# A two-layer encoder kernel: sixteen column sums as two rounded passes, later weight splits, smaller first pieces

## The chip, the cores and the metric

The kernel runs on one core of a Trainium2 chip. The time is the device time of one execution in microseconds (us). Shorter is better. A core has five engines with instruction queues of their own: TensorE (PE in the profile) multiplies matrices, VectorE (DVE) and ScalarE (ACT) do elementwise work and reductions, GpSimd (POOL) is idle here, and SyncE (SP) issues the weight transfers. PEld is the loading of a matmul's stationary operand, which overlaps PE.

## The reference

Two layers of an encoder on 272 tokens (16 learned meta tokens and 256 inputs) of width 2048. Everything is float32.

```python
def hybrid_layer(x, ...):
    h = rms_norm(x, norm_w)
    proj = jnp.einsum('bld,dn->bln', h, w_in)
    (aq, ak, av, ag, bq, bk, bv, bg, cq, ckv, ckr, cg, du, dg) = jnp.split(proj, split_points, axis=-1)
    ya = diff_attention(aq, ak, av, ...)      # A: 4 heads, two softmax maps each
    yb = axial_gqa(bq, bk, bv, ...)           # B: 4 query heads, 2 key heads
    yc = latent_attention(cq, ckv, ckr, ...)  # C
    yd = multiscale_pool(du, ...)             # D
    y = jnp.concatenate([ya * silu(ag), yb * silu(bg), yc * silu(cg), yd * silu(dg)], axis=-1)
    return x + jnp.einsum('bln,nd->bld', y, w_out)
```

What the change touches is in branch A, where every half head (64 of the 128 features of a tile) of q and k is normalized before the rotation:

```python
def rms_norm(x, w):
    y = x32 * lax.rsqrt(jnp.mean(x32 * x32, axis=-1, keepdims=True) + EPS)

q = rms_norm(q_raw.reshape(b, l, A_HEADS, 2, A_QK_DIM), q_norm_w)
k = rms_norm(k_raw.reshape(b, l, A_HEADS, 2, A_QK_DIM), k_norm_w)
...
p = softmax32(jnp.einsum('bqhmd,bkhmd->bhmqk', qb, k), scale)
w = p[:, :, 0] - lam * p[:, :, 1]
o = einsum('bhqk,bkhd->bqhd', w, v);   o = rms_norm(o, subln_w) * (1.0 - lambda_init)
```

## The kernel before

Everything is kept transposed: features on the 128 partitions, tokens along the free axis (272 columns, or 256 in the layer that no longer needs the meta tokens). Weights stream from memory in chunks of 128 x 1024 float32 (512 KB) in the order of their use. A layer has 129 slots with a chunk each, the two layers 258. Four chunks make a pair of output tiles, a chunk holding 4 k-tiles of 128 rows for both.

A product of float32 precision is made of three rounded passes. ACT rounds a chunk to `w_hi` (`split`, L1039), DVE subtracts to get `w_lo` (`split`, L1348), and PE runs for each k-tile and output tile hi·hi (L736), x-low·w-high (L737) and x-high·w-low (L738), 24 matmuls to a chunk. There are 3 raw buffers and 4 of `w_hi` and `w_lo` each. A chunk's matmuls wait for both halves of its split, and its transfer into a raw buffer waits for the `w_lo` of the chunk three before.

Between the chunks PE does what attention needs: scores (`score`, L907), transposes of probabilities (`p_turn`, L922 and L926), products with v (`pv`, L943), sums of squares down the partitions (`rope_stat` L862 and others; `sub_stat` L951). A finished tile is taken by ACT (`lift`, L1066) and scaled by DVE (`rescale`, L1356). A tile of aq or ak is then squared by ACT (`rope_pre`, L1111), summed by PE (`rope_stat`, one matmul of the float32 squares with the constant `halves`, which the trace records as x2), turned by DVE meanwhile (`rope_turn`, L1388 to L1393), and multiplied by the inverse root, which ACT makes in two steps (L1138, L1140) and DVE applies (`rope_fin`, L1431). An attention step n has on DVE its maximum (`s_max`, L1508 and L1509) and its scaling (`s_scale`, from L1517), on ACT its two exponentials (`s_exp`, L1207) and the copies of turned probabilities (`p_out`, L1220 and L1222). The heads' outputs are normalized by `sub_pre`, `sub_stat` and `sub_fin` (L1454, L1456), and split again by `y_split` (L1438).

Each engine runs its instructions in an order fixed when the kernel is built. `make_plan` gives every stage a place, its slot plus the number for its kind in `AT_TENSOR`, `AT_SCALAR` or `AT_VECTOR` (plus an exception from `MOVED`), and sorts by it. An engine that has to wait for one stage waits with all the stages behind it.

At the start SP issues chunk 0 in two halves, alternating with the first two halves of a quarter of x, then chunks 1 to 3 in whole. ACT and DVE split the first half of chunk 0 (`split_half`), then two k-tiles of x (`x_half`: `h_hi` L1020, `h_lo` L1328), and so on; `x_first` brings k-tiles 4 to 7, 8 to 11 and 12 to 15.

Of the kernel before, what the change touches and what calls it, by code (L numbers as in the profile page):

```python
# [140 lines left out]

def make_plan(at_engine):
# [8 lines left out]
    for n in (0, 1):  # L151
        plan += [(-11, 2 * n, ("split_half", n)), (-11, 2 * n + 1, ("x_half", n))]
# [4 lines left out]
    plan += [(-5, 0, ("x_first", 0, 1)), (-3, 0, ("x_first", 0, 2)), (2.9, 0, ("x_first", 0, 3))]  # L157
# [4 lines left out]
    for l in range(DEPTH):  # L162
# [105 lines left out]
def build(nc, xt, w_stream, params, lam_rows, consts, out):  # L268
# [31 lines left out]
    sq = sb("sq", [128, 4, L])  # L300
    rn = sb("rn", [128, L])
# [197 lines left out]
    for stg in vector_plan:  # L499
# [7 lines left out]
        if stg[0] == "sq_sum":  # L507
# [219 lines left out]
    def _(pe):  # L727
# [965 lines left out]
```

## Time and profile before

| | |
|---|---|
| median of 3 runs | 904.98 us (904.94 to 906.03) |
| the profiled execution's own time | 905.02 us |
| its span | 903.24 us |
| granted TensorE clock | 0.999 of full speed |
| PE busy | 895.9 us, 99% of the span |
| DVE busy | 639.5 us, 71% |
| ACT busy | 566.5 us, 63% |
| DMA | 143.8 MB, a mean of 159 GB/s |

The span is the stretch from the first to the last recorded instruction of the profiled execution; 1.8 us of its time lie around it. Matmuls are pipelined: a dense one is recorded as 0.29 us, but the next starts some 0.125 us later. So what a matmul costs is read from the starts of its neighbours and not from its own duration. Times in a timeline count from the start of the span.

### The profile page before, as it was taken

How to read it: one execution, taken by the hardware profiler on the slowest of the kernel's cores; microseconds unless marked ns; L12 is line 12 of the kernel's file. 1: busy time of each engine (PE TensorE's matmuls, PEld its weight loads, DVE VectorE, ACT ScalarE, POOL GpSimd, SP SyncE). 2: the span in 40 equal slices, each digit the busy share in tenths (PEclk: the TensorE clock that was granted, in tenths of full speed). 3: DMA queues.
4: the chain of work that ended last, by engine and by line, in shares of the span. 5: the costliest groups of instructions: out<-in, count | busy, mean ns of one | idle time of the engine just before them, and what ended most of it. 6: DMA issues, size and time to landing. Idle time of an engine off the chain costs nothing.

```text
span 903.2 us, 18071 instructions
## 1 busy us (share of the span) xinstructions
PE 895.9 (99%) x7070; PEld 860.0 (95%) x7070; DVE 639.5 (71%) x1074; ACT 566.5 (63%) x986; POOL 0.2 (0%) x4
## 2 busy tenths in 40 slices
PE   8999999999999999999999999999999999999998
PEld 7999998998999999999999999999999999999998
DVE  7785887778777776766665659887687667766552
ACT  7678756577666667745454588556686666665331
POOL 0000000000000000000000000000000000000000
PEclk9999999999999999999999999999999999999999
DMA  8754333343434443445455544334435344445561
GB/s 333 264 197 140 134 140 137 124 136 115 145 139 143 139 149 130 147 147 190 172 199 186 188 176 151 118 120 176 149 97 184 140 141 157 152 158 187 187 217 64
DMA packets 22996, 143.83 MB, mean 159 GB/s; under 512 B 2560, under 2 KB 4736, under 8 KB 6528
## 3 DMA queue, kind: packets, MB, share of 16 engines
q1 hardware_dynamic: 22768, 142.64, 44.4%
q8 instruction: 56, 0.92, 0.4%
q14 instruction: 28, 0.23, 0.1%
q10 hardware_dynamic: 144, 0.04, 0.1%
HBM read 140.58 MB, written 2.10 MB: 158 GB/s over the span
## 4 chain that ended last, share of the span: by engine, by line
PE 97%; ACT 1%; DMA 1%; SPq 0%; DVE 0%; issue 0%; ACTq 0%; DVEq 0%
PE dense L736 27%; PE dense L738 26%; PE dense L737 26%; PE s_ps L907 4%; PE o_ps L943 4%; PE norm_ps L862 2%; PE t_ps L922 2%; DMA raw<-w_stream_dram 1%; ACT w_hi L1039 1%; PE swap_ps L738 0%; PE norm_ps L738 0%; PE norm_ps L737 0%; PE swap_ps L737 0%; PE swap_ps L736 0%; PE norm_ps L736 0%; PE norm_ps L951 0%
## 5 line engine op out<-in xcount | busy, mean ns | idle before, releaser
L736 PE MATMUL dense<-h_hi,w_hi 128*128 128x272 f32 (+2 forms) x1440 | 427.1, 297 | 2.3 <-DVE h_lo L1328 2.3
L738 PE MATMUL dense<-h_hi,w_lo 128*128 128x272 f32 (+2 forms) x1440 | 412.7, 287 | 0.0
L737 PE MATMUL dense<-h_lo,w_hi 128*128 128x272 f32 (+2 forms) x1440 | 410.9, 285 | 0.0
L1348 DVE TENSOR_TENSOR w_lo<-raw,w_hi 128x1024 fp32r<-128x1024 f32 (+1 forms) x256 | 312.0, 1219 | 86.5 <-ACT w_hi L1039 80.3
L1039 ACT ACTIVATE w_hi<-raw 128x1024 fp32r<-128x1024 f32 (+1 forms) x256 | 270.3, 1056 | 70.4 <-PE dense L738 56.1
L736 PEld LDWEIGHTS dense<-h_hi,w_hi 128*128 128x128 f32 x1440 | 271.3, 188 | 7.9 <-issue 2.8
L737 PEld LDWEIGHTS dense<-h_lo,w_hi 128*128 128x128 f32 x1440 | 271.4, 188 | 1.2
L738 PEld LDWEIGHTS dense<-h_hi,w_lo 128*128 128x128 f32 x1440 | 271.1, 188 | 0.0
L736 PE MATMUL dense<-y_hi,w_hi 128*128 128x272 f32 (+1 forms) x500 | 143.6, 287 | 0.2
L738 PE MATMUL dense<-y_hi,w_lo 128*128 128x272 f32 (+1 forms) x500 | 142.7, 285 | 0.0
L737 PE MATMUL dense<-y_lo,w_hi 128*128 128x272 f32 (+1 forms) x500 | 142.4, 285 | 0.0
L736 PEld LDWEIGHTS dense<-y_hi,w_hi 128*128 128x128 f32 x500 | 94.3, 189 | 1.4 <-ACT q_st L1090 0.6
L738 PEld LDWEIGHTS dense<-y_hi,w_lo 128*128 128x128 f32 x500 | 94.3, 189 | 0.0
L737 PEld LDWEIGHTS dense<-y_lo,w_hi 128*128 128x128 f32 x500 | 94.1, 188 | 0.0
L1066 ACT ACTIVATE row<-dense 128x272 f32<-128x272 f32 (+2 forms) x80 | 31.5, 394 | 71.5 <-PE dense L738 70.8
L1508 DVE TENSOR_REDUCE stat<-s_ps 128x1 f32<-128x272 f32 (+1 forms) x80 | 35.1, 439 | 35.1 <-PE s_ps L907 33.1
L1356 DVE TENSOR_TENSOR row<-row,rinv 128x272 f32<-128x272 f32 (+2 forms) x80 | 34.9, 437 | 28.4 <-ACT row L1066 26.6
L1138 ACT ACTIVATE rn<-norm_ps,eps_c 128x272 f32<-128x272 f32 (+1 forms) x50 | 24.2, 484 | 42.0 <-PE norm_ps L862 30.0
L1207 ACT ACTIVATE probs<-s_ps,stat 128x272 f32<-128x272 f32 (+1 forms) x80 | 38.9, 486 | 14.0 <-DVE stat L1509 11.6
L1337 DVE TENSOR_TENSOR x<-x,dense 128x272 f32<-128x272 f32 (+1 forms) x28 | 12.0, 429 | 46.7 <-PE dense L738 46.7
L943 PE MATMUL o_ps<-p_t,v_st 128*128 128x128 f32 (+1 forms) x288 | 38.2, 278 | 0.3 <-ACT p_t L1222 0.3
L907 PE MATMUL s_ps<-k_st,q_st 64*128 64x272 f32 (+1 forms) x240 | 37.6, 417 | 0.0
(175 smaller groups left out, 808.1 us busy)
## 6 DMA issues: line engine op xcount, KB each, us to landing
raw<-w_stream_dram SPq DMA_DIRECT2D x128, 1024.0 KB, 4.8
out_dram<-x SPq DMA_DIRECT2D x8, 256.0 KB, 4.7
x<-xt_dram SPq DMA_DIRECT2D x3, 544.0 KB, 8.9
raw<-w_stream_dram SPq DMA_DIRECT2D x3, 512.0 KB, 7.6
con<-consts_dram SPq DMA_DIRECT2D x1, 984.0 KB, 7.8
x<-xt_dram SPq DMA_DIRECT2D x2, 272.0 KB, 4.8
raw<-w_stream_dram SPq DMA_DIRECT2D x2, 256.0 KB, 4.6
d_w<-consts_dram SPq DMA_DIRECT2D x2, 256.0 KB, 5.3
```

What stands on the lines that cost most here:

```text
L736: nc.tensor.matmul(ps, whi, xhi, start=first, stop=False)
L737: nc.tensor.matmul(ps, whi, xlo, start=False, stop=False)
L738: return nc.tensor.matmul(ps, wlo, xhi, start=False, stop=last)
L907: mm = nc.tensor.matmul(s_ps[m][0:nq, 0:L], queries[half, q:q + nq], keys[half, :], start=n_part == 0, stop=n_part == len(parts) - 1)
L943: mm = nc.tensor.matmul(o_ps[:, c:c + nq], v_st[:, b, v_columns(vh)], p_t[:, 4 if b == 2 else 2 * m + b, 0:nq], start=b == 0, stop=b == 2)
L1039: signal(nc.scalar.activation(w_hi[:, g % RING, 0:n], raw[:, e % RAW, CHUNK * half:CHUNK * half + n], ACT.Copy), hi_ready, g + 1)
L1066: signal(nc.scalar.activation(tile_place(l, p, j), ps[:, 0:L - tile_from(l, kind, j)], ACT.Copy), lifted, scaled_no[(l, p, j)])
L1138: signal(nc.scalar.activation(rn[:, t0:L], norm_ps[:, t0:L], ACT.Ln, scale=1.0 / width, bias=eps_c[:, 0:1]), norm_taken, n + 1)
L1207: signal(nc.scalar.activation(probs[0:nq, k % 2, m, :], s_ps[m][0:nq, 0:L], ACT.Exp, bias=stat[0:nq, 2 + m:3 + m], scale=SCALE[b], accum_o ...
L1348: signal(nc.vector.tensor_tensor(w_lo[:, g % RING, 0:n], raw[:, e % RAW, CHUNK * half:CHUNK * half + n], w_hi[:, g % RING, 0:n].bitcast(F3 ...
L1356: signal(nc.vector.tensor_tensor(out_, out_, rinv[:, tile_from(l, PAIRS[p][0], j):L], ALU.mult), scaled, scaled_no[(l, p, j)])
L1508: link(nc.vector.reduce_max(stat[0:nq, m:m + 1], s_ps[m][0:nq, 0:L], AX.X))
```

## The change

**The sums.** The 16 sums of aq and ak (4 tiles each in 2 layers) are made from two rounded parts. ACT copies the squares to a rounded `sq_hi` behind the square, DVE subtracts to get `sq_lo` (a new stage `sq_low` at place 0.6), and PE runs two passes over a rounded copy of `halves`, one slot later than the single sum stood. `rope_fin` is one slot later too, and `sub_slot` keeps the sums of head outputs out of the two slots in which these now stand.

**Copies of probabilities.** `p_out` on ACT goes from place 0.56 to 0.105, directly ahead of `rope_pre` (0.11).

**Late weight splits.** On DVE the `split` of slots 27 to 94 of each layer goes from 0.71 to 1 + 0.491 + 0.03, behind the `s_scale` of the slot after.

**The start.** Chunk 0 is transferred and split in k-tiles 0, 1 and 2-3. The first quarter of x comes in the same pieces and is issued by ACT, ahead of its table load; SP issues weights and the rest of x. `x_first` is cut finer.

```diff
+FIRST = [(0, 1), (1, 2), (2, 4)]
...
-                 y_split=0.66, xscale=0.283, sub_pre=0.439, x_out=0.55, p_out=0.56, gate=0.65, s_exp=0.579,
+                 y_split=0.66, xscale=0.283, sub_pre=0.439, x_out=0.55, p_out=0.105, gate=0.65, s_exp=0.579,
...
-AT_VECTOR = dict(sq_sum=0.2, rope_mid=0.25, rope_turn=0.65, s_max=-0.418, lam_dot=-0.35, sub_fin=-0.345, rope_fin=-0.34, lat_fin=0.055, head_out=0.17,
+AT_VECTOR = dict(sq_sum=0.2, sq_low=0.6, rope_mid=0.25, rope_turn=0.65, s_max=-0.418, lam_dot=-0.35, sub_fin=-0.345, rope_fin=-0.34, lat_fin=0.055, head_out=0.17,
...
+LATE_SPLITS = (27, 95)
...
-            plan.append((slot + at_engine[kind] + MOVED.get(stage, 0), len(plan), stage))
+            place = at_engine[kind] + MOVED.get(stage, 0)
+            if kind == "split" and at_engine is AT_VECTOR and LATE_SPLITS[0] <= stage[2] < LATE_SPLITS[1]:
+                place = 1 + at_engine["s_scale"] + 0.03
+            plan.append((slot + place, len(plan), stage))
...
-    plan += [(-5, 0, ("x_first", 0, 1)), (-3, 0, ("x_first", 0, 2)), (2.9, 0, ("x_first", 0, 3))]
+    plan += [(-6.5, 0, ("x_first", 4, 6)), (-5, 0, ("x_first", 6, 8)), (-3, 0, ("x_first", 8, 12)),
+             (2.9, 0, ("x_first", 12, 16))]
...
-                    at(s, ("rope_stat", l, kind, i0 + j))
-                    at(s + 1, ("rope_fin", l, kind, i0 + j))
+                    at(s, ("sq_low", "rope", l, kind, i0 + j))
+                    at(s + 1, ("rope_stat", l, kind, i0 + j))
+                    at(s + 2, ("rope_fin", l, kind, i0 + j))
...
-            taken |= {pair_slot(p) + 4, pair_slot(p) + 5}
+            taken |= {pair_slot(p) + 5, pair_slot(p) + 6}
...
-            sp.dma_start(x[:, 2 * n:2 * n + 2, :], xt[:, 2 * n:2 * n + 2, :]).then_inc(s_x[0] if n else s_x_half, 16)
...
+            if key not in ("aq", "ak"):
+                sums = nc.tensor.matmul(norm_ps[:, t0:L], halves, sq[:, 2 * half, t0:L], start=True, stop=True)
             else:
...
+                nc.tensor.matmul(norm_ps[:, t0:L], sums_of[:, :], sq_hi[:, half, t0:L], start=True, stop=False)
+                sums = nc.tensor.matmul(norm_ps[:, t0:L], sums_of[:, :], sq_lo[:, half, t0:L], start=False, stop=True)
...
+            act.dma_start(x[:, 0:1, :], xt[:, 0:1, :]).then_inc(s_x_part[0], 16)
             act.dma_start(par[:, :], params).then_inc(s_par, 16)
+            act.dma_start(x[:, 1:2, :], xt[:, 1:2, :]).then_inc(s_x_part[1], 16)
+            act.dma_start(x[:, 2:4, :], xt[:, 2:4, :]).then_inc(s_x[0], 16)
             nc.scalar.preload_act_table_set("natural_log_exp_and_others")
...
+            signal(nc.scalar.activation(sq_hi[:, half, t0:L], sq[:, 2 * half, t0:L], ACT.Copy), pre_done,
                    pre_no[("rope_pre", l, key, i)])
...
+        def sq_low(what, l, key, i):
+
+            t0, half = rope_from(l, key), parity("rope_stat", l, key, i)
+            dve.wait_ge(pre_done, pre_no[("rope_pre", l, key, i)])
+            signal(nc.vector.tensor_tensor(sq_lo[:, half, t0:L], sq[:, 2 * half, t0:L],
+                                           sq_hi[:, half, t0:L].bitcast(F32), ALU.subtract), summed,
+                   sum_no[(what, l, key, i)])
```

Three places show what moved. **DVE in layer 0, slots 58 to 61, before.** `w_lo<-raw,w_hi` is a weight split, the 16-row lines are an attention step's, the `tab` and `k_st` lines turn and scale the tile ak3. From the split of chunk 60 on:

```order
L1348 TENSOR_TENSOR w_lo<-raw,w_hi 128x1024
L1508 TENSOR_REDUCE stat<-s_ps 16x1 x2
L1509 TENSOR_SCALAR stat<-stat 16x2
L1388 STREAM_SHUFFLE tab<-row 128x272
L1389 SCALAR_TENSOR_TENSOR tab<-tab,par,con 128x272
L1391 SCALAR_TENSOR_TENSOR k_st<-row,par,con 128x272
L1393 TENSOR_TENSOR k_st<-k_st,tab 128x272
L1431 TENSOR_TENSOR k_st<-k_st,rn 128x272
L1348 TENSOR_TENSOR w_lo<-raw,w_hi 128x1024
L1517 RECIPROCAL stat<-stat 16x2
```

After, from the same split on:

```order
L1377 TENSOR_TENSOR w_lo<-raw,w_hi 128x1024
L1545 TENSOR_REDUCE stat<-s_ps 16x1 x2
L1546 TENSOR_SCALAR stat<-stat 16x2
L1409 TENSOR_TENSOR sq_lo<-sq,sq_hi 128x272
L1425 STREAM_SHUFFLE tab<-row 128x272
...
L1468 TENSOR_TENSOR k_st<-k_st,rn 128x272
L1554 RECIPROCAL stat<-stat 16x2
L1557 TENSOR_TENSOR stat<-stat,neg_lam 16x1
L1558 TENSOR_SCALAR probs<-probs,stat 16x272
L1559 SCALAR_TENSOR_TENSOR probs<-probs,stat 16x272
L1377 TENSOR_TENSOR w_lo<-raw,w_hi 128x1024
```

The split of chunk 61, the last line of the second list, now stands behind the four scaling instructions of the attention step, and there is a subtraction more ahead of it. The split of chunk 59 has moved in the same way behind the scaling of the step before.

**DVE in layer 1, slot 79, before.** The `tab` and `yt` lines are the normalization of a head's output, `sq<-sq` adds the squares of two bq tiles and the four lines behind it begin their rotation (chunk 208 is this layer's slot 79):

```order
L1356 TENSOR_TENSOR row<-row,rinv 128x256 x2
L1454 SCALAR_TENSOR_TENSOR tab<-o_ps,sub_w,rn 128x256
L1456 TENSOR_TENSOR yt<-tab,g_st 128x256
L1348 TENSOR_TENSOR w_lo<-raw,w_hi 128x1024
L1374 TENSOR_TENSOR sq<-sq 128x256
L1404 SCALAR_TENSOR_TENSOR tab<-row,par,con 128x2x256
L1405 SCALAR_TENSOR_TENSOR q_st<-row,par,con 128x2x256
L1407 TENSOR_TENSOR q_st<-q_st,tab 128x2x256
```

After:

```order
L1385 TENSOR_TENSOR row<-row,rinv 128x256 x2
L1491 SCALAR_TENSOR_TENSOR tab<-o_ps,sub_w,rn 128x256
L1493 TENSOR_TENSOR yt<-tab,g_st 128x256
L1403 TENSOR_TENSOR sq<-sq 128x256
L1441 SCALAR_TENSOR_TENSOR tab<-row,par,con 128x2x256
L1442 SCALAR_TENSOR_TENSOR q_st<-row,par,con 128x2x256
L1444 TENSOR_TENSOR q_st<-q_st,tab 128x2x256
L1377 TENSOR_TENSOR w_lo<-raw,w_hi 128x1024
```

The split of chunk 208 has gone from directly behind the head's output to behind the sum and the rotation.

**ACT at the start, before:**

```order
L977 DMA par<-params_dram 128x84
L978 ACT_TABLE_LOAD
L983 ACTIVATE w_hi<-raw 128x512
L1020 ACTIVATE h_hi<-x,par 128x272 x2
L983 ACTIVATE w_hi<-raw 128x512
L1020 ACTIVATE h_hi<-x,par 128x272 x2
L989 ACTIVATE w_hi<-raw 128x512 x2
L1039 ACTIVATE w_hi<-raw 128x1024
L1020 ACTIVATE h_hi<-x,par 128x272 x4
```

After:

```order
L998 DMA x<-xt_dram 128x544
L999 ACT_TABLE_LOAD
L1004 ACTIVATE w_hi<-raw 128x256
L1044 ACTIVATE h_hi<-x,par 128x272
L1004 ACTIVATE w_hi<-raw 128x256
L1044 ACTIVATE h_hi<-x,par 128x272
L1004 ACTIVATE w_hi<-raw 128x512
L1044 ACTIVATE h_hi<-x,par 128x272 x2
L1011 ACTIVATE w_hi<-raw 128x512 x2
L1044 ACTIVATE h_hi<-x,par 128x272 x2
L1063 ACTIVATE w_hi<-raw 128x1024
L1044 ACTIVATE h_hi<-x,par 128x272 x2
```

Three transfers more are issued ahead of the table load (the last is shown), the first split covers one k-tile in place of two, and two of the four k-tiles of x that stood behind the split of chunk 2 (L1039, now L1063) stand ahead of it.

## Rows read from the trace of the kernel before

**Rows 1.** Page, part 4: the chain that ended last, share of the span by engine

```profile
PE 97%; ACT 1%; DMA 1%; SPq 0%; DVE 0%; issue 0%; ACTq 0%; DVEq 0%
```

**Rows 2.** Waits of PE: waiting tile, waited-for line, us in total, times, longest

```profile
PE dense L736 <- DVE h_lo L1328: 2.3, 3, 1.7
```

**Rows 3.** PE timeline, 272 columns wide: start, duration, engine, line, operation, tiles

```profile
89.76 0.29 PE L738 MATMUL dense<-h_hi,w_lo 128*128 128x272 f32 x1
89.89 0.62 PE L862 MATMUL norm_ps<-sq,con 128*128 128x272 f32 x2
...
90.47 0.28 PE L737 MATMUL dense<-h_lo,w_hi 128*128 128x272 f32 x1
```

**Rows 4.** PE timeline, 256 wide, at chunk 208

```profile
743.83 0.28 PE L738 MATMUL dense<-h_hi,w_lo 128*128 128x256 f32 x1
...
744.19 0.47 PE L736 MATMUL dense<-h_hi,w_hi 128*128 128x256 f32 x1
744.50 0.28 PE L737 MATMUL dense<-h_lo,w_hi 128*128 128x256 f32 x1
```

**Rows 5.** PE timeline of the start, around the two pauses

```profile
9.07 0.36 PE L736 MATMUL dense<-h_hi,w_hi 128*128 128x272 f32 x1 [0.17 <-DVE h_lo L1328]
...
13.55 0.29 PE L738 MATMUL o_ps<-h_hi,w_lo 128*128 128x272 f32 x1
14.25 0.36 PE L736 MATMUL dense<-h_hi,w_hi 128*128 128x272 f32 x1 [0.41 <-DVE h_lo L1328]
```

**Rows 6.** ACT timeline of the start: chunk 2's rounding

```profile
11.18 1.06 ACT L1039 ACTIVATE w_hi<-raw 128x1024 fp32r<-128x1024 f32 x1 [1.15 <-DMA raw<-w_stream_dram]
```

**Rows 7.** DVE timeline of the start: the low parts of x tiles 4 to 7

```profile
13.60 2.11 DVE L1328 SCALAR_TENSOR_TENSOR h_lo<-x,par,h_hi 128x272 fp32r<-128x272 f32 x4
```

**Rows 8.** Page, part 6: transfers, count, KB each, us from issue to landing

```profile
raw<-w_stream_dram SPq DMA_DIRECT2D x2, 256.0 KB, 4.6
```

**Rows 9.** DVE timeline, layer 0: from the scaling of step 10 to chunk 61's split

```profile
220.92 0.17 DVE L1517 RECIPROCAL stat<-stat 128x2 f32<-128x2 f32 x1
...
222.26 0.46 DVE L1388 STREAM_SHUFFLE tab<-row 128x272 f32<-128x272 f32 x1
...
224.31 0.44 DVE L1431 TENSOR_TENSOR k_st<-k_st,rn 128x272 f32<-128x272 f32 x1
224.79 1.22 DVE L1348 TENSOR_TENSOR w_lo<-raw,w_hi 128x1024 fp32r<-128x1024 f32 x1
226.04 0.89 DVE L1508 TENSOR_REDUCE stat<-s_ps 16x1 f32<-16x272 f32 x2
...
227.17 0.46 DVE L1388 STREAM_SHUFFLE tab<-row 128x272 f32<-128x272 f32 x1
...
229.69 1.23 DVE L1348 TENSOR_TENSOR w_lo<-raw,w_hi 128x1024 fp32r<-128x1024 f32 x1
```

**Rows 10.** ACT timeline at the same place: the second exponential, and the square

```profile
220.17 0.49 ACT L1207 ACTIVATE probs<-s_ps,stat 128x272 f32<-128x272 f32 x1
...
222.85 0.43 ACT L1111 ACTIVATE sq<-row 128x272 f32<-128x272 f32 x1
```

**Rows 11.** PE timeline: the first matmul of chunk 61

```profile
232.50 0.39 PE L736 MATMUL dense<-h_hi,w_hi 128*128 128x272 f32 x1
```

**Rows 12.** DVE timeline, layer 1: the maximum of step 7

```profile
668.93 0.17 DVE L1509 TENSOR_SCALAR stat<-stat 128x2 f32<-128x2 f32 x1
```

**Rows 13.** PE timeline: the first matmul of chunk 189

```profile
678.02 0.37 PE L736 MATMUL dense<-h_hi,w_hi 128*128 128x272 f32 x1
```

**Rows 14.** DVE timeline, layer 1: splits around the rotation, chunk 208's first

```profile
741.60 1.23 DVE L1348 TENSOR_TENSOR w_lo<-raw,w_hi 128x1024 fp32r<-128x1024 f32 x1
...
745.62 1.23 DVE L1348 TENSOR_TENSOR w_lo<-raw,w_hi 128x1024 fp32r<-128x1024 f32 x1
```

**Rows 15.** PE timeline: the probabilities' product that waits, and one that doesn't

```profile
769.71 1.60 PE L943 MATMUL o_ps<-p_t,v_st 128*128 128x128 f32 x12 [0.28 <-ACT p_t L1222]
...
794.55 1.50 PE L943 MATMUL o_ps<-p_t,v_st 128*128 128x128 f32 x12
```

More of the change, by code:

```diff
@@ L300, in build @@
     sq = sb("sq", [128, 4, L])
+    sums_of = sb("sums_of", [128, 128], F32R)
+    sq_hi = sb("sq_hi", [128, 2, L], F32R)
+    sq_lo = sb("sq_lo", [128, 2, L], F32R)
     rn = sb("rn", [128, L])
@@ L685, in _ @@
     def _(sp):
-        for n in (0, 1):
-            at = slice(CHUNK // 2 * n, CHUNK // 2 * n + CHUNK // 2)
-            sp.dma_start(raw[:, 0, at], w_stream[0, :, at]).then_inc(s_first[0] if n else s_half, 16)
-            sp.dma_start(x[:, 2 * n:2 * n + 2, :], xt[:, 2 * n:2 * n + 2, :]).then_inc(s_x[0] if n else s_x_half, 16)
+        for n, (a, b) in enumerate(FIRST):
+            at = slice(256 * a, 256 * b)
+            sp.dma_start(raw[:, 0, at], w_stream[0, :, at]).then_inc((*s_part, s_first[0])[n], 16)
         for c in range(1, 4):
@@ L856, in rope_stat @@
             t0 = rope_from(l, key)
-            if key in PAIRED:
+            if key in ("kr", "qr"):
+                pe.wait_ge(pre_done, pre_no[("rope_pre", l, key, i)])
+            else:
                 pe.wait_ge(summed, sum_no[("rope", l, key, i)])
-            else:
-                pe.wait_ge(pre_done, pre_no[("rope_pre", l, key, i)])
-            norm_free("rope_stat", l, key, i)
-            sums = nc.tensor.matmul(norm_ps[:, t0:L], halves, sq[:, 2 * parity("rope_stat", l, key, i), t0:L],
-                                    start=True, stop=True)
+            norm_free("rope_stat", l, key, i)
+            half = parity("rope_stat", l, key, i)
+            if key not in ("aq", "ak"):
+                sums = nc.tensor.matmul(norm_ps[:, t0:L], halves, sq[:, 2 * half, t0:L], start=True, stop=True)
+            else:
+                if (l, key, i) == (0, "aq", 0):
+                    pe.wait_ge(ones_ready, 1)
+                nc.tensor.matmul(norm_ps[:, t0:L], sums_of[:, :], sq_hi[:, half, t0:L], start=True, stop=False)
+                sums = nc.tensor.matmul(norm_ps[:, t0:L], sums_of[:, :], sq_lo[:, half, t0:L], start=False, stop=True)
             sums.then_inc(stat_done, 1)
@@ L1010, in lambda_exp @@
             signal(nc.scalar.activation(lam_sum[:, :], lam_sum[:, :], ACT.Exp), lam_exp, 1)
+            act.wait_ge(s_const, 16)
+            nc.scalar.activation(sums_of[:, :], halves, ACT.Copy).then_inc(ones_ready, 1)
         def x_tile(l, kt):
@@ L1110, in rope_pre @@
                 return
-            signal(nc.scalar.activation(sq[:, 2 * half, t0:L], rope_source(key, i)[:, t0:L], ACT.Square), pre_done,
+            square = nc.scalar.activation(sq[:, 2 * half, t0:L], rope_source(key, i)[:, t0:L], ACT.Square)
+            if key in ("kr", "qr"):
+                signal(square, pre_done, pre_no[("rope_pre", l, key, i)])
+                return
+            link(square)
+            signal(nc.scalar.activation(sq_hi[:, half, t0:L], sq[:, 2 * half, t0:L], ACT.Copy), pre_done,
                    pre_no[("rope_pre", l, key, i)])
@@ L1270, in second_half, with x_part, x_first @@
                    (second_lo, lo_ready)[n], 1 + n)
-        def x_half(n):
+        def x_part(n):
             if n == 0:
                 dve.wait_ge(s_par, 16)
-            dve.wait_ge((s_x_half, s_x[0])[n], 16)
-            for kt in (2 * n, 2 * n + 1):
+            dve.wait_ge((*s_x_part, s_x[0])[n], 16)
+            for kt in range(*FIRST[n]):
                 x_lo(0, kt)
-        def x_first(_, c):
-            dve.wait_ge(s_x[c], 16)
-            for kt in range(4 * c, 4 * c + 4):
+        def x_first(a, b):
+            dve.wait_ge(s_x[a // 4], 16)
+            for kt in range(a, b):
                 x_lo(0, kt)
```

52 lines of the change are left out of this document (27 added, 25 removed).

## The prediction

> **What bounds the kernel now.** I read the chain of work first: 97% of it is PE [rows 1]. Then PE's waits, to see what is left to win on them: 2.3 us for low parts of x, all in the first 15 us [rows 2], and single waits of 0.3 us or less [rows 15]. So the kernel is bound by PE's own stream. It becomes faster only where PE has less to run or where one of these few waits goes, and slower where another engine makes PE wait. DVE and ACT have idle time (71% and 63% busy), but a share says nothing of the stage in which one of them is late. So I compared, for every chunk, the end of its `w_lo` on DVE with its first matmul. The lead is 4 to 5 us for most, but small for some: chunk 61's split starts at 229.69 and ends 1.6 us ahead of its first matmul at 232.50 [rows 9, 11]. What the change puts ahead of that split decides whether PE waits there.
>
> **The sums, on PE.** A single sum stands between two dense matmuls. From the L738 at 89.76 to the L737 at 90.47 there are 0.71 us, two dense steps of 0.125 and the sum: 0.46 us [rows 3]. At 256 columns it is 744.50 - 743.83 = 0.67 less two steps of 0.117 (no row shows a pair of them here; it is 0.125 x 256/272), so 0.43 [rows 4]. The two rounded passes have the form of dense matmuls, so I price them at two dense steps, 0.25 and 0.235. That saves 0.21 for each of the 12 wide sums and 0.19 for each of the 4 narrow ones (aq in layer 1): 2.5 + 0.8 = **-3.3 us**, all on the path. Bounds: the matmul behind a change of form starts late (0.31 instead of 0.125 from 744.19 to 744.50 [rows 4]), which the single sum pays already. If the two passes pay as much, 16 x 0.15 = 2.4 of it are lost, so -0.9; if neither they nor their neighbours pay, -4.5. The nearest row is the dense pair, so I keep -3.3.
>
> **The start.** PE waits at 9.07 and 14.25 [rows 5]. The second pause has a clear cause: chunk 2's weights land at 11.18, ACT rounds 1.06 and DVE splits 1.23 [rows 6, 9], to about 13.55, and only then does DVE start the low parts of x tiles 4 to 7, at 0.53 each [rows 7]. PE, which needs one in each 0.375 us (three dense steps), waits for the first (14.25 - 13.55 = 0.70 instead of 0.125, so 0.6 lost [rows 5]) and 0.16 for each of the three others: 1.05 in all. After the change two of these tiles are split ahead of chunk 2's split, which takes that away unless the chunk lands later; what then remains is the split itself, done at 13.6. PE's first matmul comes somewhat sooner because one k-tile is split in place of two (a fourth of a chunk less on each of ACT and DVE, 0.3 each), but then it only meets the landing of the next pieces. I take **-1.0 us** for the whole start. Bounds: -1.5 (both), and +0.5, since nine transfers are now in flight where seven were and par stands behind a piece of x. A half chunk takes 4.6 us to land [rows 8]; the smaller pieces are not in the trace.
> The Trainium skill ("DMA: Bandwidth & Descriptors", section "Issuing engines are not separate DMA queues") says that issuing from several engines only saves the sequencer's time for the issue, since all run on the same 16 DMA engines. By that rule, moving x to ACT brings no transfer forward by more than the issues ahead of it. Whether it holds at the start no row decides; with it the start would be worth less than I take. The sum doesn't use it.
>
> **Copies of probabilities ahead of squares.** At 769.71 PE waits for a copy of turned probabilities, which on ACT stands behind a square. The pv group there takes 771.07 - 769.15 = 1.9 us against 1.3 to 1.4 at 794.55 [rows 15], measured from the last dense matmul ahead to the first one behind. With the copy ahead of the square the wait goes: **-0.5**. Two smaller waits of the kind (for a head's output at 576, a turn at 232) give **-0.2**. Bounds 0 and -0.8. What is pushed back is the square, and behind it at chunk 87 the sum and the rotation on DVE: +0.2 by the walk below.
>
> **The rounding added on ACT and DVE.** 16 copies and 16 subtractions, each priced as the square, 0.43, or as a 272-column subtraction, 0.44 with 0.04 to the next [rows 9, 10]: 7 us more on each engine, none on the path in itself. They are hidden under PE's chunks as long as the leads last.
>
> **The late splits.** They bring nothing that this trace shows: no attention work of DVE holds PE before, so moving splits behind `s_scale` frees no wait. They cost where the lead was small. I walked DVE's new order by hand from the trace's starts: s_scale 220.92 to 222.26 = 1.34; rotation 222.26 to 224.31 = 2.05; final product 0.48; split 1.25; maximum of two 226.04 to 227.17 = 1.13 [rows 9]; new subtraction 0.47. PE's own times in the walk have the saved sums taken out.
> 1. *Chunk 61, layer 0.* The exponentials of step 10 end at 220.74 [rows 10] and after the change at about 220.85: a sum moved behind chunk 56 lets ACT start 0.9 earlier, copies and a square that now stand ahead take it back. DVE, which before ran the split of chunk 59 in that time, now waits for them, as the split stands behind. Then come s_scale 1.34, split 59 1.25, subtraction 0.47, rotation 2.05, low part of y 0.47, split 60 1.25, maximum 1.13, subtraction 0.47, rotation and final product 2.53, s_scale 1.3, split 61 1.25: 13.5 us, to 234.4. PE would be there at 232.50 less four sums' savings, 0.84: 231.65 [rows 11]. **+2.8**. Half of it is already met at the subtraction of ak3 (ready at 229.3, PE there at 227.95).
> 2. *Chunk 189, layer 1.* The same pattern. The maximum of step 7 ends at 669.1 [rows 12]; two subtractions more ahead of it, less some idle, make it 669.8. Exponentials 1.23, s_scale 1.34, split 188 1.25 and the subtraction for ak2 0.47 end at 674.1, where PE is ready at 672.75. So 1.4 there, and chunk 189 starts at 678.8 where it would at 677.2 (678.02 less the savings) [rows 13]: **+1.5**.
> 3. *Chunk 208.* Its split started at 741.60; now the sum and the rotation, 745.62 - 741.60 - 1.26 = 2.76, stand ahead of it [rows 14]. It ends at 745.6 instead of 742.8, and the first matmul stood at 744.19 [rows 4]: **+1.4**.
> 4. *Chunk 200*, the same with a later start: **+0.35**. Elsewhere (chunks 28 to 46, 63 to 86, 157 to 184, 209 to 223) the leads hold by 0.4 us or more.
>
> Sum of the stalls with chunk 87: 2.8 + 1.5 + 1.4 + 0.35 + 0.2 = **+6.3**. Bounds: 0, if DVE waits less for exponentials than I walked and the leads absorb the rest, and +9, if the backlog of one place carries to the next where I left 0.4.
>
> **The sum.** -3.3 - 1.0 - 0.5 - 0.2 + 6.3 = +1.3. The profiled execution took 905.02 (span 903.24 and 1.8 around it), the median is 904.98, so the two agree. 905.0 + 1.3 = **906.3 us**.
>
> **The rivals.**
> *All gains and hardly a stall.* DVE does not fall behind at the four places: the chains above hold the stalls in a sum of 12 terms, and if ACT reaches step 10's exponentials some 2.5 us sooner (its work before is ordered anew too, and it has idle time for that), chunk 61 doesn't wait; the same slack would do for chunks 189 and 208. For it: DVE is 71% busy and the median lead is 4 to 5 us. Against it: for chunk 208 the walk has only three terms and starts from a wait on PE's own work. Left are -5.0 and about +0.5 at chunks 200 and 208: 900.5. Chance 0.2.
> *Half the stalls.* One of the two large ones is real, as PE's delay at the first gives DVE time for what follows: 905.0 - 5.0 + 3.2 = 903.2. Chance 0.2.
> *The backlog spreads.* This one ends clearly slower. A raw buffer is refilled only after its `w_lo`, and a split that comes 0.8 of a slot later delays the transfer; ACT then rounds late and DVE's next split waits. It decides when the delay exceeds what a transfer has in hand, 4.6 us of landing [rows 8] against some 10 us of three chunks. With +2 more of stall, 908.3. With the start worth nothing, 909. Chance 0.2.
> *The two passes save little.* If each pass pays for the change of form, -0.9 instead of -3.3, and with my stalls 908.7. Chance 0.05 beside the others.
>
> **How the numbers follow.** My sum with +-1.5 has 0.35, the rivals 0.2, 0.2, 0.2 and 0.05. A measurement here can tell 0.2%, 1.8 us, from no change: faster is below 903.2, slower above 906.8. Faster has the first rival and half the second, 0.3. Slower has the third and fourth and a third of my case, 0.36. The rest, 0.34, is within. The likeliest single case is 906.3 with its own range 904.8 to 907.8. The range that leaves out 2 in 10 reaches from the first rival's 900.5 to 908.6.
>
> **What would show it.** Right: between dense matmuls the two sums take 0.25 us; PE shows waits at chunk 61 and 189 of over 1 us each, put down to `w_lo` or `sq_lo`, and one at chunk 208; DVE waits for step 10's exponentials near 219; no wait for `p_t` near 769. The pause at 14.25 is gone. Wrong: PE's waits sum to under 1 us behind the first 15 us (first rival), PE waits for `w_hi` or a transfer (third), or the sums take 0.4 (fourth).

## The result

The changed kernel takes 911.69 us in the median of 5 executions (909.64 to 912.46), against 905.04 for the kernel before (904.94 to 906.03): a ratio of 1.0069 by their means, with a 95% interval of 1.0056 to 1.0083. It is 6.6 us slower by the medians. The forecast was 906.3 in a range of 900.5 to 908.6, so the time is 3 us beyond the upper end. The profiled execution took 912.03 us with a span of 910.1. The mean granted TensorE clock, which is given for each execution, was 1.0 in the fastest of the five, 0.999 in the one at 911.69, and 0.996 in the other three. Later, one execution of the kernel before and one of `pause_short` took 3074 us and are left out of every ratio.

The page after, its lines for the clock and the chain, the second of which answers to [rows 1]:

```profile
PEclk8999999999999999999999999999999999999999
PE 91%; DVE 4%; ACT 3%; DMA 1%; issue 1%; ACTq 0%; DVEq 0%
```

PE's share of the chain fell from 97% to 91%, DVE and ACT took 7% of it, and in the first of 40 slices the granted clock is below nine tenths. PE's waits (waiting tile, waited-for line, us in total, times, longest) answer to [rows 2]:

```profile
PE dense L748 <- DVE h_lo L1357: 2.5, 3, 1.8
PE norm_ps L880 <- DVE sq_lo L1409: 2.5, 2, 1.3
PE dense L748 <- DVE w_lo L1377: 2.3, 3, 1.1
PE t_ps L940 <- DVE probs L1559: 0.3, 1, 0.3
```

Two waits for the new `sq_lo` and three for a weight split are new. To see where the 6.8 us between the two traces come from, I subtracted the start of each of the 258 chunks in the trace before from its start in the trace after, and looked at where the difference changes:

| place | change of the lag, us | forecast |
|---|---|---|
| start, up to chunk 16 | +3.5 | -1.0 |
| 16 sums (measured in `low_on_pool`, below) | -3.1 | -3.3 |
| chunks 60 and 61 | +2.8 | +2.8 |
| chunks 188 to 190 | +1.9 | +1.5 |
| chunk 208 | +1.4 | +1.4 |
| chunks 87 and 200 | +0.6 | +0.55 |
| smaller waits in front of chunks 43, 58, 186 and 216 | +0.5 to 0.8 | 0 |
| the probabilities' waits | -0.7 | -0.7 |

The rows add up to 6.9 to 7.2, a little over the 6.8. So the stalls and gains behind the start came nearly as walked. The start did not.

### The profile page after: what moved, and what is told of

Same layout as the page of the kernel before. It is cut to its first block, busy times and chain, and to the rows that moved or that the text cites. A ratio compares the mean times of both kernels' runs of the same rounds, so it can differ in the third digit from the quotient of the medians.

```text
span 910.1 us, 18130 instructions
## 1 busy us (share of the span) xinstructions
PE 897.3 (99%) x7070; PEld 861.1 (95%) x7070; DVE 646.6 (71%) x1091; ACT 573.9 (63%) x1004; POOL 0.2 (0%) x4
## 4 chain that ended last, share of the span: by engine, by line
PE 91%; DVE 4%; ACT 3%; DMA 1%; issue 1%; ACTq 0%; DVEq 0%
PE dense L748 25%; PE dense L750 25%; PE dense L749 25%; PE s_ps L925 4%; PE o_ps L961 3%; PE t_ps L940 1%; DVE w_lo L1377 1%; PE norm_ps L876 1%; ACT w_hi L1063 1%; DMA x<-xt_dram 1%; PE swap_ps L750 0%; PE norm_ps L750 0%; PE norm_ps L749 0%; PE swap_ps L749 0%; PE swap_ps L748 0%
## 5 line engine op out<-in xcount | busy, mean ns | idle before, releaser
L1063 ACT ACTIVATE w_hi<-raw 128x1024 fp32r<-128x1024 f32 (+1 forms) x256 | 270.3, 1056 | 70.7 <-PE dense L750 57.6
```

The costliest lines, as they stand in the source:

```text
L1063: signal(nc.scalar.activation(w_hi[:, g % RING, 0:n], raw[:, e % RAW, CHUNK * half:CHUNK * half + n], ACT.Copy), hi_ready, g + 1)
```

## Experiments: the parts

**The start of before.** The rest of the change is kept, the halves and the one queue of before are back:

```diff
-        for n, (a, b) in enumerate(FIRST):
-            at = slice(256 * a, 256 * b)
-            sp.dma_start(raw[:, 0, at], w_stream[0, :, at]).then_inc((*s_part, s_first[0])[n], 16)
+        for n in (0, 1):
+            at = slice(CHUNK // 2 * n, CHUNK // 2 * n + CHUNK // 2)
+            sp.dma_start(raw[:, 0, at], w_stream[0, :, at]).then_inc(s_first[0] if n else s_half, 16)
+            sp.dma_start(x[:, 2 * n:2 * n + 2, :], xt[:, 2 * n:2 * n + 2, :]).then_inc(s_x[0] if n else s_x_half, 16)
...
-            act.dma_start(x[:, 0:1, :], xt[:, 0:1, :]).then_inc(s_x_part[0], 16)
```

> The changed kernel with the start of before (halves of chunk 0, x issued by SP). In the trace of the changed kernel chunk 3 starts 3.3 us later than before, and the last chunk 6.8, so behind the start 3.5 are lost. If the start is a loss of its own, the time is 911.7 - 3.4 = 908.3 us. If the rest would stall as long anyway because PE comes to DVE's late splits sooner (rival), some of the gain is lost and it stays above 910.

908.23 us (1.0035, 1.0023 to 1.0048), as expected. The start is a loss of its own, 3.5 us, and what is left is 3.1 us slower than before.

**The start alone**, the other way round:

> The kernel before with the changed start alone. Theory (late landing of x's second piece, and the lower clock behind it): 905.0 + 3.4 = 908.4 us, with PE idle near 8 us and a granted clock under 0.9 in the first 20 us. Rival (the low clock is an accident of that run, not of the start): within 1 us of 905 + 0.7.

908.66 us (1.0033, 1.0021 to 1.0044), with the lower clock in the profiled execution (0.55 of full speed on average from 9.9 to 17 us). So both ways agree. Its seven executions lie at 906.5 and 906.9, both with a mean granted clock of 1.0, and at 908.4 to 909.1, with 0.996 to 0.998; that gap comes back below.

**The late splits alone:**

```diff
+LATE_SPLITS = (27, 95)
...
+            if kind == "split" and at_engine is AT_VECTOR and LATE_SPLITS[0] <= stage[2] < LATE_SPLITS[1]:
+                place = 1 + at_engine["s_scale"] + 0.03
```

> The kernel before with the late splits of slots 27 to 94 alone. Walk: chunk 208 waits 1.4 us, chunk 61 some 1.2 (two subtractions less in its chain, and PE not yet 0.8 sooner), chunk 200 0.3, chunk 87 none: 908 us. Rival (the late splits cost nothing, it was the subtractions): 905.0 to 905.5.

907.48 us (1.0026, 1.0016 to 1.0036). The theory holds: chunk 61 comes 0.95 us later, chunk 208 1.45, chunk 200 0.35, and nothing comes sooner but one turn by 0.21. The late splits cost 2.4 us by themselves.

**Sums and copies without late splits**, with the start of before:

```diff
-LATE_SPLITS = (27, 95)
+LATE_SPLITS = (0, 0)
```

> Two-pass sums and early copies only: start of before and splits at their old place. Theory: the gains stay and the stalls go, 905.0 - 3.3 - 0.6 = 901.1 us. Rival (the 14 us of added rounding on ACT and DVE stall PE by themselves): 903 or more.

904.34 us (0.9997, 0.9988 to 1.0005): no difference from before that can be measured, where 901.1 was expected. My theory of these parts was wrong by 3 us, and the time is the rival's (903 or more); that the added roundings are the reason is only partly so, as the traces show. PE's longest wait in its trace, and the two-pass sum that I had priced at 0.25 us:

```profile
232.62 0.29 PE L939 MATMUL t_ps<-con,probs 16*128 16x16 f32 x2 [1.53 <-DVE probs L1554]
...
149.96 0.29 PE L749 MATMUL dense<-h_hi,w_lo 128*128 128x272 f32 x1
150.09 0.29 PE L879 MATMUL norm_ps<-sq_hi,sums_of 128*128 128x272 f32 x1
150.21 0.29 PE L880 MATMUL norm_ps<-sq_lo,sums_of 128*128 128x272 f32 x1
150.34 0.83 PE L960 MATMUL o_ps<-p_t,v_st 128*128 128x128 f32 x6
```

The two passes take 150.34 - 150.09 = 0.25 us, just the price of two dense ones, against 0.46 in [rows 3]. So the sums are cheap. About half of what is lost is lost in one wait: ahead of 232.6 PE wants to turn the probabilities of step 11, which DVE has not scaled. A second wait of this kind at 666 costs 0.4 us, and the rest are small delays ahead of sums and chunks. From 213 to 234 us DVE has no idle time at all, as it had none in the trace before from 212 to 237 us. There the turn came just in time. PE's last dense matmul ahead of the turn, and the end of DVE's scaling, first before, then here:

```profile
231.93 0.29 PE L738 MATMUL dense<-h_hi,w_lo 128*128 128x272 f32 x1
231.71 0.49 DVE L1522 SCALAR_TENSOR_TENSOR probs<-probs,stat 16x272 f32<-16x272 f32 x1
```

```profile
230.81 0.29 PE L749 MATMUL dense<-h_hi,w_lo 128*128 128x272 f32 x1
232.08 0.49 DVE L1554 SCALAR_TENSOR_TENSOR probs<-probs,stat 16x272 f32<-16x272 f32 x1
```

PE is there 1.1 us sooner, and DVE is done 0.4 us later (232.57 instead of 232.20). So most of the wait is PE's own gain, which DVE's chain doesn't follow, and the smaller part is DVE's added work.

**Late splits away from the stalls.** `old_start` again, but the splits of the slots where the trace shows stalls are at their old place:

```diff
+KEPT = {(0, 59), (0, 60), (0, 61), (1, 57), (1, 58), (1, 59), (1, 60), (0, 71), (1, 71), (0, 79), (1, 79), (0, 87), (1, 87)}
...
-            if kind == "split" and at_engine is AT_VECTOR and LATE_SPLITS[0] <= stage[2] < LATE_SPLITS[1]:
+            if kind == "split" and at_engine is AT_VECTOR and LATE_SPLITS[0] <= stage[2] < LATE_SPLITS[1] and stage[1:] not in KEPT:
```

> old_start with the late splits everywhere but at the slots 59 to 61, 57 to 60 of layer 1, 71, 79 and 87. Theory (the late splits cost only where a lead was short, and bring nothing elsewhere): 904.3 us, as old_start_no_late. Rival (they help elsewhere): below 903.9. Rival (the backlog spreads): above 905.

906.62 us (1.0011, 1.0002 to 1.0019), with executions at 905.1 to 905.5 and at 906.5 to 906.8. None is below 905.0, so the late splits bring nothing elsewhere; the first group is some 1.0 us above the lower one of `old_start_no_late`, as a subtraction of squares at 229 comes 0.5 us late behind the late splits ahead of it and two smaller waits remain. The rival of a spreading backlog has something to it, at a small size.

**The copies alone** (`p_out` from 0.56 to 0.105, nothing else):

> The kernel before with the copies of probabilities at place 0.105 alone. Theory: the wait at 769.7 goes, 905.1 - 0.5 = 904.6 us. Rival (squares that stand behind the copies come late for a sum): 905.1 or more.

904.87 us (0.9997, 0.9989 to 1.0006). In the trace PE's stretch with the probabilities' product near 769 is 0.54 us shorter, as forecast; 0.2 of it are lost at another place, at chunk 170. By the times the difference can't be told from none.

## Experiments: what holds PE near 232 us

**The subtractions on GpSimd.** DVE's 16 `sq_low` go to the idle engine, with `old_start_no_late` as the base:

```diff
+    @block.gpsimd
+    def _(pool_engine):
+        for stage, *what in vector_plan:
+            if stage == "sq_low":
+                _, l, key, i = what
+                t0, half = rope_from(l, key), parity("rope_stat", l, key, i)
+                pool_engine.wait_ge(pre_done, pre_no[("rope_pre", l, key, i)])
+                nc.gpsimd.tensor_tensor(sq_lo[:, half, t0:L], sq[:, 2 * half, t0:L],
+                                        sq_hi[:, half, t0:L].bitcast(F32), ALU.subtract).then_inc(low_done, 1)
```

> old_start_no_late with the 16 subtractions of squares on the idle GpSimd instead of DVE. Theory (from 213 to 234 us DVE has no idle time, so its two added subtractions, 0.9 us, and PE's earlier arrival, 0.8, come back as the wait of 1.5 us for the step's probabilities at 232.6): that wait shrinks to 0.7 us or less, waits for sq_lo go, no run falls to a lower clock behind it, 903.0 us (902.5 to 903.5). Rival (ACT's copies are to blame): 904.3 as before, the wait stays at 1.5.

902.89 us (0.9975, 0.9965 to 0.9984), 2.3 us faster than before and, with `scale_sooner` below, the fastest kernel of this study. The small delays ahead of the sums and the second wait for probabilities are gone, and so is the upper group of times (9 executions from 902.7 to 903.1). But the first wait for the probabilities shrank by 0.2 us only:

```profile
PE t_ps L942 <- DVE probs L1549: 1.3, 1, 1.3
...
L1574 POOL TENSOR_TENSOR sq_lo<-sq,sq_hi 128x272 fp32r<-128x272 f32 (+1 forms) x16 | 15.7, 982 | 657.0 <-ACT sq_hi L1138 657.0
```

Why so little? PE's last dense matmul and DVE's scaling ahead of the turn, and one of DVE's instructions beside GpSimd:

```profile
230.52 0.29 PE L751 MATMUL dense<-h_hi,w_lo 128*128 128x272 f32 x1
231.56 0.49 DVE L1549 SCALAR_TENSOR_TENSOR probs<-probs,stat 16x272 f32<-16x272 f32 x1
```

```profile
223.24 0.89 DVE L1420 TENSOR_TENSOR k_st<-k_st,tab 128x272 f32<-128x272 f32 x1
```

DVE is done 0.5 us sooner and not 0.9, because the instruction of the last line takes 0.89 us while GpSimd subtracts, where it took 0.44; and PE is there 0.3 us sooner still. Against the kernel before, PE is now 1.4 us sooner and DVE 0.15: without any added instruction on DVE, PE's gain is still lost here.
The span is 2.2 us shorter than before. Take away the 1.3 that step 11 costs and the 0.5 of the probabilities' product, and add the 0.2 that this execution lost at its start: the 16 sums bring 3.1 us, 0.19 each. That term of the forecast was right.

**DVE's order at step 11.** Its scaling goes ahead of the final product of ak2 and of the split of chunk 61 (`("s_scale", 0, 11): -0.836` in `MOVED`), and in a second kernel that final product goes behind the split too (`rope_fin` of (0, ak, 2) on DVE at +0.06). Base: `low_on_pool`.

> low_on_pool with DVE's scaling of step 11 ahead of the final product of ak2 and of the split of chunk 61. Theory (the wait of 1.3 us is DVE's order): the wait for probabilities goes, chunk 61 waits for its w_lo instead, some 1.0 us; 902.6 us. Rival (ACT or PE sets it): 902.9 unchanged, the wait stays on the probabilities.

> As scale_sooner, with that final product on DVE behind the split of chunk 61 too. Theory: chunk 61 waits 0.5 us, 902.1 us. Rival (ACT, which waits for the final product before its next inverse root, and with it the lift of a tile, comes late): 902.6 or more.

They took 902.93 us (0.9975, 0.9966 to 0.9985) and 905.47 us (1.0002, 0.9993 to 1.0011). In the first the wait for the probabilities went, but PE then waited as long at chunk 61, and not for its `w_lo`. In the second that wait grew:

```profile
PE dense L749 <- ACT row L1088: 1.4, 1, 1.4
```

```profile
232.28 0.49 ACT L1167 ACTIVATE rn<-norm_ps,eps_c 128x272 f32<-128x272 f32 x1 [2.83 <-DVE k_st L1460]
...
233.81 0.36 PE L751 MATMUL dense<-h_hi,w_hi 128*128 128x272 f32 x1 [2.64 <-ACT row L1090]
```

The first line is PE's wait in `scale_sooner`, the other two are ACT's and PE's timeline in `scale_sooner_fin_later`. They show a chain that I had not seen: chunk 61 needs a bank of the memory that PE writes to, and ACT frees it by lifting a tile (`row`). The lift stands on ACT behind the inverse root of ak3, which waits for DVE to take that of ak2 (one `rn` buffer). The change put `rope_fin` one slot later, so that this pair now stands ahead of the lift. So three things meet within half a microsecond: the scaling, the split and the lift. Moving one only shows the next. Part of my theory held (the wait went to chunk 61), the release was another than I had named; for the second kernel the rival named this chain, and was right. That kernel too has groups of times: 3 executions at 904.2 to 904.3, 7 at 905.4 to 905.8 and one at 906.5. The traced one, at 904.31, is of the lowest.

## Experiments: the start

PE at the start of the changed kernel (timeline; the row at 9.37 answers to that at 9.07 in [rows 5]), and ACT:

```profile
7.29 0.29 PE L750 MATMUL dense<-h_hi,w_lo 128*128 128x272 f32 x1
9.37 0.57 PE L748 MATMUL dense<-h_hi,w_hi 128*128 128x272 f32 x1 [1.79 <-DVE h_lo L1357]
9.74 0.43 PE L749 MATMUL dense<-h_lo,w_hi 128*128 128x272 f32 x1
9.96 0.43 PE L750 MATMUL dense<-h_hi,w_lo 128*128 128x272 f32 x1
...
16.03 0.29 PE L750 MATMUL t_ps<-h_hi,w_lo 128*128 128x272 f32 x1
16.16 0.28 PE L748 MATMUL t_ps<-h_hi,w_hi 128*128 128x272 f32 x1
```

```profile
8.07 0.52 ACT L1044 ACTIVATE h_hi<-x,par 128x272 fp32r<-128x272 f32 x1 [1.80 <-DMA x<-xt_dram]
...
10.06 1.08 ACT L1044 ACTIVATE h_hi<-x,par 128x272 fp32r<-128x272 f32 x2 [0.81 <-DMA x<-xt_dram]
```

The first matmul came at 6.59 instead of 7.15. Then the second k-tile of x was missing until 8.07, PE paused, and from 9.37 to 16.03 its matmuls started 0.227 us apart instead of 0.125: the clock stood at the lower of its two levels (1.2 instead of 2.4 GHz). Two losses, then: x comes late, and the clock falls around the pause (the granted clock is at half from 9.2 to 16.0). The fastest execution of the changed kernel, 909.64 us with a clock of 1.0, is still 1.4 us above `old_start`.

**Pieces in one queue, and halves in two.** The one keeps the three pieces and lets SP issue x's in turn with the weights'. The other keeps the halves and lets ACT issue x's two, with par between:

```diff
             sp.dma_start(raw[:, 0, at], w_stream[0, :, at]).then_inc((*s_part, s_first[0])[n], 16)
+            sp.dma_start(x[:, a:b, :], xt[:, a:b, :]).then_inc((*s_x_part, s_x[0])[n], 16)
```

```diff
+            act.dma_start(x[:, 0:2, :], xt[:, 0:2, :]).then_inc(s_x_half, 16)
             act.dma_start(par[:, :], params).then_inc(s_par, 16)
+            act.dma_start(x[:, 2:4, :], xt[:, 2:4, :]).then_inc(s_x[0], 16)
```

> The changed start with its three pieces, but x's pieces issued by SP in turn with the weights', as before. Theory (x is late because the weights of chunk 1 on SP's queue overtake it): no pause over 1 us, no fall of the clock, 904.5 to 905.3 us. Rival (small pieces land late by themselves): above 907.

> The kernel before, in halves as before, with x's two halves issued by ACT around par. Theory (the second queue delays x): x's second half lands later than 8.4, a pause of PE of 1 us or more, 906 to 908.5 us. Rival (it is the pieces): 905 us or a little less.

906.93 us (1.0018, 1.0009 to 1.0027) and 907.15 us (1.0022, 1.0013 to 1.0031). I had expected the queue alone to be guilty. Each of the two costs 1.7 to 1.9 us. The transfers (count, KB each, median us from issue to landing), first in halves in two queues, then in pieces in one:

```profile
x<-xt_dram ACTq DMA_DIRECT2D x2, 272.0 KB, 6.7
raw<-w_stream_dram SPq DMA_DIRECT2D x2, 256.0 KB, 5.8
par<-params_dram ACTq DMA_DIRECT2D x1, 42.0 KB, 6.6
```

```profile
raw<-w_stream_dram SPq DMA_DIRECT2D x3, 1024.0 KB, 11.2
raw<-w_stream_dram SPq DMA_DIRECT2D x3, 512.0 KB, 8.8
x<-xt_dram SPq DMA_DIRECT2D x2, 136.0 KB, 3.7
raw<-w_stream_dram SPq DMA_DIRECT2D x2, 128.0 KB, 2.8
```

With two queues everything that is urgent lands later: x's halves in 6.7 us where they took 4.8 in one queue, a half chunk in 5.8 where [rows 8] has 4.6. SP, which no longer issues x, starts the next chunks sooner, and they share the DMA engines with x. The Trainium skill ("DMA: Bandwidth & Descriptors", section "Issuing engines are not separate DMA queues") says that transfers of different issuing engines run on the same 16 DMA engines and interleave. These rows agree. I had named the rule and left it out of the sum.
The late landing is not all of it. In `halves_two_queues` ACT's first rounding of x waited last for par, which stands between x's halves in ACT's queue, and PE then ran at the slow pace from its first dense matmul at 9.13 to 14.5:

```profile
7.83 1.08 ACT L1021 ACTIVATE h_hi<-x,par 128x272 fp32r<-128x272 f32 x2 [1.25 <-DMA par<-params_dram]
```

```profile
9.13 0.57 PE L735 MATMUL dense<-h_hi,w_hi 128*128 128x272 f32 x1 [2.75 <-DVE h_lo L1329]
```

What the place of par costs by itself, and what the second queue would cost with the clock up, no run separates.
With the pieces, the first two do land sooner (2.8 and 3.7 us; the first matmul starts at 5.79), but the large transfers behind them later: whole chunks take 8.8 us instead of 7.6, pairs of chunks 11.2 instead of 9.1. Chunk 2 was rounded from 13.33 instead of 11.18 [rows 6], and started 1.5 us later. Whether the two more issues of SP or the shorter rows of the pieces are to blame I did not separate.

**PE kept busy.** To part the late x from the clock, matmuls on zeros are put ahead of the second and the third k-tile, in `start_only`:

```diff
+                if k == 1 or k == 2:
+                    for _ in range(14 if k == 1 else 8):
+                        nc.tensor.matmul(s_ps[0][:, 0:L], g_st[:, 0, 0:128], g_st[:, 1, :], start=True, stop=True)
```

> The kernel before with the changed start, and 14 and 8 matmuls on zeros (the warm-up's) put ahead of the second and the third k-tile of chunk 0, so that PE has no pause while x is late. Computes the same. Theory (of the 3.5 us of start_only about 1.5 are the late x and 2 the halved clock behind PE's pause): the granted clock stays at 1.0 and the time is 906.7 us. Rival (the clock falls for another reason, such as the transfers): the clock falls as in start_only and the time is 908.6 or more.

> start_only with 4 and 2 matmuls on zeros ahead of the second and third k-tile of chunk 0 instead of 14 and 8, which had taken 0.4 us each and held chunk 1 back by 9 us. Computes the same. Theory (the halved clock follows PE's pause): the clock stays at 1.0 in every run, all runs within 0.5 us of 906.7, none at 909. Rival (another cause for the fall): runs at 908.5 to 909.1 as in start_only.

The first took 913.84 us (1.0095, 1.0081 to 1.0108). The filling was far too long: a float32 matmul costs 0.4 us here at full clock. The clock stayed at 1.0, so the experiment says a little of the clock and nothing of the time. The second took 906.53 us (1.0020, 1.0011 to 1.0029), near the expected 906.7, but not in every run: 7 of 11 lie at 906.3 to 907.2 and 4 at 908.2 to 908.4. In the profiled execution, one of the four, already the first k-tile ran at the slow pace, before any pause that I had filled. There the ten warm-up matmuls ahead of it had run at the slow pace as well, so the clock had not yet risen (it is given as 1.0 there all the same, and only the pace of the matmuls, 0.227 us apart, tells). The lower group lies where that of `start_only` lies. What the filling may have changed is how often an execution falls into it, 7 of 11 instead of 2 of 7, and that is no proof.

**A pause far from the start.** In the kernel before, DVE repeats one subtraction ahead of the split of chunk 239, in a stretch of dense matmuls, 5 or 7 times:

```diff
+            for _ in range(7 if (l, s) == (1, 110) else 0):
+                link(nc.vector.tensor_tensor(w_lo[:, g % RING, 0:n], raw[:, e % RAW, CHUNK * half:CHUNK * half + n],
+                                             w_hi[:, g % RING, 0:n].bitcast(F32), ALU.subtract))
```

> The kernel before with 5 more copies of one subtraction on DVE, ahead of the split of chunk 239, in a quiet stretch of dense matmuls near 846 us. Computes the same. The split leads by 5.84 us there and 5 x 1.26 are 6.3, so PE pauses 0.5 us. Both theories: 905.1 + 0.5 = 905.6 us, clock 1.0.

> The same with 7 copies, 8.8 us, so PE pauses 3.0 us. Theory (a pause of PE halves the clock for some us behind it, without anything else happening): matmuls behind it start 0.23 us apart instead of 0.12, about 1.5 to 2 us more, 909.8 us. Rival (the pause costs its own length only): 908.1 us.

910.74 us (1.0064, 1.0051 to 1.0078) and 913.77 us (1.0095, 1.0081 to 1.0109). The profiled execution of `pause_short` is an odd one, 912.52 us with a mean clock of 0.947, where the others lie at 910.3 to 910.7 with 0.998; its slow stretch behind the pause is seen all the same, from 849.4 to 852.1. The pauses became longer than I had worked out, 3.7 and 6.3 us, because PE waited for an addition (L1337) queued behind the repeated subtractions, and not for the split. That spoils the comparison of a short pause with a long one. What the clock does can still be read. PE's wait in `pause_long`, and three stretches, the first of them still in the pause (PE busy, PEld, DVE, ACT, POOL with counts, then the granted clock, DMA share, GB/s):

```profile
PE dense L736 <- DVE x L1337: 6.3, 1, 6.3
```

```profile
848.40:850.00 1.60, 0.07 (x1) 0.10 (x1) 1.53 (x3) 0.00 (x0) 0.00 (x0) 0.50 0.00 0
850.00:855.00 5.00, 5.00 (x24) 5.00 (x25) 2.68 (x3) 0.00 (x0) 0.00 (x0) 0.50 0.81 259
855.00:860.00 5.00, 5.00 (x43) 5.00 (x43) 1.73 (x2) 2.12 (x2) 0.00 (x0) 0.98 0.39 164
```

24 matmuls in 5 us at half the clock, 43 at the full one. From 849.9 to 855.2 they start 0.21 us apart instead of 0.12, which costs 2.4 us. 6.3 + 2.4 = 8.7, and the kernel is 8.6 us slower by its median. So a pause of PE alone, 800 us away from the start's transfers, halves the clock behind it. The theory holds against the rival of a pause that costs its own length only. It holds against the transfers as the cause too: the clock is at half from 848.4 on, inside the pause, and until 850.0 the DMA engines move nothing.

The same is seen in `late_but_stalls` without any such construction, behind a wait of 1.5 us:

```profile
233.29 0.29 PE L940 MATMUL t_ps<-con,probs 16*128 16x16 f32 x2 [1.52 <-DVE probs L1555]
...
234.65 0.34 PE L750 MATMUL dense<-h_hi,w_lo 128*128 128x272 f32 x1
234.78 0.43 PE L748 MATMUL dense<-h_hi,w_hi 128*128 128x272 f32 x1
235.01 0.43 PE L749 MATMUL dense<-h_lo,w_hi 128*128 128x272 f32 x1
235.24 0.43 PE L750 MATMUL dense<-h_hi,w_lo 128*128 128x272 f32 x1
...
239.16 0.29 PE L750 MATMUL dense<-h_hi,w_lo 128*128 128x272 f32 x1
```

The matmuls run at full pace for 1.4 us more, then at half pace for 3.4, and chunk 62 is 1.5 us late. It does not happen every time: the traced execution of `old_start_no_late` has a wait of 1.53 us and that of `scale_sooner_fin_later` one of 2.64, and both ran on at full pace. That fits the groups of times. `old_start_no_late` has 7 executions at 904.0 to 904.3, all with a mean granted clock of 1.0, and 4 at 905.6 to 905.9, with 0.997 to 0.998. `scale_sooner_fin_later` has 0.999 or 1.0 in its lowest three and 0.997 to 0.998 in the others. `low_on_pool`, with a wait of 1.3, has all 9 at 902.7 to 903.1 and none under 0.999. I have a trace of only one execution of each, so in which stretch the clock fell in the upper groups is inferred.

## Why the prediction failed, step by step

- **What bounds the kernel, and where DVE is close behind:** right. The chain and PE's waits led to the right four places, with the right releasers:

```profile
232.29 0.40 PE L880 MATMUL norm_ps<-sq_hi,sums_of 128*128 128x272 f32 x1 [1.26 <-DVE sq_lo L1409]
...
237.36 0.40 PE L748 MATMUL dense<-h_hi,w_hi 128*128 128x272 f32 x1 [0.94 <-DVE w_lo L1377]
...
751.43 0.39 PE L748 MATMUL dense<-h_hi,w_hi 128*128 128x256 f32 x1 [1.10 <-DVE w_lo L1377]
```

  These are the sum ahead of chunk 60, chunk 61 [rows 11] and chunk 208 [rows 4] in the changed kernel. "Half of it is already met at the subtraction of ak3" was borne out too.
- **The walk of DVE:** right in its mechanism and nearly in its size. DVE idles for step 10's exponentials, as forecast, and the new order puts the split of chunk 61 13.5 us behind them (223.8 to 237.3):

```profile
223.83 0.17 DVE L1554 RECIPROCAL stat<-stat 128x2 f32<-128x2 f32 x1 [0.98 <-ACT probs L1236]
...
231.79 0.44 DVE L1409 TENSOR_TENSOR sq_lo<-sq,sq_hi 128x272 fp32r<-128x272 f32 x1
...
236.08 1.23 DVE L1377 TENSOR_TENSOR w_lo<-raw,w_hi 128x1024 fp32r<-128x1024 f32 x1
```

  Forecast +6.3, measured 7.2 to 7.5. The rest are small waits in front of chunks 43, 58, 186 and 216, where I had taken leads of 0.4 us to be enough.
- **Where the cost sits:** partly wrong. I had given nearly the whole 6.3 us to the late splits. Taking them out saved 3.9 (908.2 to 904.3), and alone they cost 2.4. At the turn ahead of chunk 61 a wait of 1.5 us remains without them: PE comes 1.1 us sooner, and DVE is done 0.4 later. The step that failed here is "7 us more on each engine, none on the path in itself". With the subtractions on GpSimd the kernel is 1.4 us faster, so on DVE they did cost; but the larger part of the wait is a gain of PE in a stretch where DVE had no idle time to follow it. In the sum of the whole change this did not show, since the walk held both.
- **The sums,** -3.3: measured -3.1. **The probabilities,** -0.7: measured -0.7 in the traces.
- **The start,** -1.0 with a bound of +0.5: measured +3.5. This is the step that failed in the forecast. It failed twice. I priced the engines' work (a quarter chunk less to split) and took the transfers' landing times as given, though at this point the DMA engines are what everything waits for: a second queue let weights that nobody needed yet share them with x (and put par behind a piece of x). And I priced a pause of PE at its length. Behind a pause the clock can fall, and the executions of `start_only` with and without the fall differ by about 2 us. With +3.5 in place of -1.0 the sum is 910.8 us, within the 909.6 to 912.5 of the executions; the stalls, measured some 1 us above the walk, make up the rest to the median.
- **The rivals:** none had this. The pages of the profile had a hint: the start's transfers take 4.6 to 9 us for pieces of 0.25 to 1 MB, and the mean busy share of the DMA engines was 0.9 in the first 20 us.

## What to carry to other kernels

At a start that waits for memory, do not ask what a smaller piece saves on the engines, but which bytes land later for it. A second issuing queue takes the order away that one queue had given. Price a wait of TensorE at more than its length where it may bring the clock down, and compare several executions: two groups of times for one kernel, with different mean clocks, point to it. Before adding even half a microsecond to an engine that is 71% busy, look at the stretch in which it lands. In a stretch without idle time an addition can come back as a wait, and so can what PE itself gains ahead of it. There the addition belongs on an idle engine, though that is not free either: with the subtractions on GpSimd and the late splits and the new start left out, this change is worth 2.3 us.

## What the runs showed of the hardware

A TensorE pause of 1.5 us in the middle of a dense stretch was followed, 1.4 us after its end, by 3.4 us at half the clock (`late_but_stalls`), one of 6.3 us by 5.3 us at half the clock at once (`pause_long`). Pauses of 1.53 and 2.64 us in other traces were followed by no such stretch (`old_start_no_late`, `scale_sooner_fin_later`). GpSimd takes 0.8 us in the median (0.7 to 1.8) for a 272-column subtraction that costs DVE 0.44, and beside ten of its sixteen subtractions a DVE instruction took 0.2 to 0.6 us longer than its like elsewhere, such as 0.89 us in place of 0.44 (`low_on_pool`).
